# Stepping over neighbouring blocks in the moving operand and the result of the up and down projections

## What is computed

```python
# first block, feed-forward part: D_FF = 2816
h = rms_norm(x, norm_ffn_pre)
u = causal_dwconv(h @ w_up, conv_ffn_w)          # w_up: 1024 x 5632
a, g = jnp.split(u, 2, axis=-1)
f = (jax.nn.gelu(g, approximate=True) * a) @ w_down   # w_down: 2816 x 1024
x = x + rms_norm(f, norm_ffn_post)
...
# second block, feed-forward part: D_FF_2 = 4096
hn = rmsnorm(h, norm_mlp_g)
x = h + jnp.square(jax.nn.relu(hn @ w_up)) @ w_down   # 1024 x 4096 and 4096 x 1024
```

## Time and profile before

| | |
|---|---|
| time, median of 2 runs | 902.34 us (901.83 to 902.85) |
| profiled execution, first to last instruction | 900.7 us |
| PE busy | 888.3 us, 99% |
| PE weight loads busy (beside PE) | 821.5 us, 91% |
| DVE busy | 571.0 us, 63% |
| ACT busy | 496.2 us, 55% |
| POOL busy | 136.0 us, 15% |
| granted TensorE clock, mean | 1.000 |
| DMA | 156.33 MB, mean 174 GB/s |

### The profile page before, as it was taken

The page is one execution under the profiler, slowest core; times in us unless marked ns, Lnnn a source line. Parts: engine busy times, 40 slices in busy tenths (PEclk is TensorE's granted clock), DMA queues, the critical chain, the costliest instruction groups (busy, mean ns, idle before and its releaser), DMA issues.

```text
span 900.7 us, 15634 instructions
## 1 busy us (share of the span) xinstructions
PE 888.3 (99%) x6451; PEld 821.5 (91%) x6451; DVE 571.0 (63%) x824; ACT 496.2 (55%) x771; POOL 136.0 (15%) x151
## 2 busy tenths in 40 slices
PE   8999999999999999999999999999999999999998
PEld 8999999889999988788899988999999899998886
DVE  4556554878888746666767797765467655554542
ACT  5576864556656634566776764423454565554330
POOL 6011101611111100133443110000100011110000
PEclk9999999999999999999999999999999999999999
DMA  7843364665665566346544546542345656656560
GB/s 279 275 155 118 95 227 150 232 207 181 199 199 179 188 210 214 131 169 242 182 141 144 160 133 177 155 135 77 115 140 191 187 168 202 193 187 204 181 200 23
DMA packets 132594, 156.33 MB, mean 174 GB/s; under 512 B 9353, under 2 KB 106028, under 8 KB 132268
## 3 DMA queue, kind: packets, MB, share of 16 engines
q1 hardware_dynamic: 125844, 151.78, 51.9%
q10 hardware_dynamic: 6680, 3.56, 1.3%
HBM read 153.08 MB, written 2.24 MB: 172 GB/s over the span
## 4 chain that ended last, share of the span: by engine, by line
PE 83%; DVE 8%; DMA 3%; ACT 3%; issue 1%; POOL 1%; SPq 0%; ACTq 0%; POOLq 0%
PE ps L1979 72%; PE ps L1934 4%; PE ps L2010 3%; DVE wl L828 2%; PE ps L1931 2%; PE ps L2235 2%; DVE gv L862 1%; DVE gkq L862 1%; DMA U<-blocks 1%; DMA raw<-in_w_in 1%; DMA blocks<-last 1%; DVE mt L1267 1%; DMA Yc<-inverses 1%; ACT wh L1426 1%; DMA inverses<-Y 0%
## 5 line engine op out<-in xcount | busy, mean ns | idle before, releaser
L828 DVE TENSOR_TENSOR wl<-raw,wh 128x1024 fp32r<-128x1024 f32 (+1 forms) x275 | 326.4, 1205 | 190.0 <-ACT wh L1426 189.9
L1979 PE MATMUL ps<-xh,wh 128*128 128x256 f32 x1280 | 357.3, 282 | 0.7 <-ACT xh L1474 0.7
L1979 PE MATMUL ps<-xh,wl 128*128 128x256 f32 x1280 | 350.6, 277 | 0.0
L1426 ACT ACTIVATE wh<-raw 128x1024 fp32r<-128x1024 f32 (+1 forms) x292 | 286.6, 1024 | 115.4 <-PE ps L1979 93.0
L1979 PE MATMUL ps<-xl,wh 128*128 128x256 f32 x1280 | 348.3, 277 | 0.0
L1979 PEld LDWEIGHTS ps<-xh,wh 128*128 128x128 f32 x1280 | 238.9, 188 | 4.5 <-issue 1.4
L1979 PEld LDWEIGHTS ps<-xh,wl 128*128 128x128 f32 x1280 | 238.8, 188 | 0.0
L1979 PEld LDWEIGHTS ps<-xl,wh 128*128 128x128 f32 x1280 | 238.0, 188 | 0.3
L669 POOL TENSOR_TENSOR wl<-raw,wh 128x1024 fp32r<-128x1024 f32 (+1 forms) x17 | 44.2, 2600 | 81.6 <-ACT wh L1426 81.3
L1979 PE MATMUL ps<-wh,f2L 128*128 128x512 f32 x128 | 49.8, 389 | 0.0
L1979 PE MATMUL ps<-wl,f2H 128*128 128x512 f32 x128 | 49.8, 389 | 0.0
(11 more groups left out here) (334 smaller groups left out, 1363.8 us busy)
## 6 DMA issues: line engine op xcount, KB each, us to landing
raw<-in_w_in SPq DMA_DIRECT2D x55, 1024.0 KB, 5.1
raw<-in_w_up SPq DMA_DIRECT2D x38, 1024.0 KB, 5.2
raw<-in_w_down SPq DMA_DIRECT2D x26, 1024.0 KB, 5.0
raw<-in_w_out SPq DMA_DIRECT2D x8, 1024.0 KB, 5.1
raw<-in_w_proj_fox SPq DMA_DIRECT2D x4, 1024.0 KB, 5.1
raw<-in_w_proj_gdn SPq DMA_DIRECT2D x4, 1024.0 KB, 5.1
raw<-in_w_conv_branch SPq DMA_DIRECT2D x4, 512.0 KB, 3.4
raw<-in_w_att_branch SPq DMA_DIRECT2D x4, 512.0 KB, 3.3
```

Of the source, the lines that this page charges most:

```text
L828: e.tensor_tensor(L, R, H.bitcast(F32), ALU.subtract).then_inc(lo.sem)
L1426: e.activation(tile_of(WH, u)[:, k:kc, :], tile_of(RAW, u)[:, k:kc, :], ACT.Copy).then_inc(hi.sem)
L1979: k = e.matmul(o, l, r, start=opens, stop=done and n == ends[c], skip_group_check=True)
```

## The change

In the units of the four feed-forward stages the access patterns of the moving operand `r` and of the result `o` are rearranged, both in the same way: `(b h e)` becomes `h b e`. With h = 2 and e = 16, all even runs of 16 elements (64 bytes) are taken first, then all odd ones. Each column still goes to its own place.

| units | stage | h, e | runs | shape of `r` and `o` |
|---|---|---|---|---|
| 32 to 53 | first up | 2, 16 | 64 bytes | 128 x 2 x 8 x 16 |
| 54 to 62 | first down, without the last three units | 4, 16 | 64 bytes | 128 x 4 x 8 x 16 |
| 114 to 129 | second up | 2, 32 | 128 bytes | 128 x 2 x 4 x 32 |
| 130 to 145 | second down | 2, 8 | 32 bytes | 128 x 2 x 32 x 8 |

The stationary operand, the number and order of instructions on every engine, the waits and the transfers are the same as before.

```diff
@@ in tensor(e), beside unit
+            def strided(ap, h, e):
+
+                return ap.rearrange("p (b h e) -> p h b e", h=h, e=e)
+
+            def order_of(u):
+                if U_UP <= u < U_DN:
+                    return 2, 16
+                if U_DN <= u < AHEAD2[0]:
+                    return 4, 16
+                if U_UP2 <= u < U_DN2:
+                    return 2, 32
+                return (2, 8) if u >= U_DN2 else None
+
@@ in unit
                     W = (H, H, L)[j][:, q, :]
                     cs = slice(c * P, (c + 1) * P)
                     l, r = (W[:, cs], X) if mode == "B" else (X[:, cs], W)
+                    if order_of(u):
+                        o, r = strided(o, *order_of(u)), strided(r, *order_of(u))
                     k = e.matmul(o, l, r, start=opens, stop=done and n == ends[c], skip_group_check=True)
```

## The result

The changed kernel takes 920.57 us (median of 2 runs, 920.25 to 920.88) against 902.34, a ratio of 1.0202 with a 95% interval of 1.0173 to 1.0232. It is 18.2 us slower. That it is slower is clear; whether by more than two per cent is not, since 2% lies inside the interval. The time lies in the stated range, but the forecast was no change.

A forecast was written before the change was run, and what follows sets the result against it. TensorE's matmul pace was taken to bound the kernel. The 900.7 us span plus 337.3 us of touched matmuls times a pace change of zero, with 1.6 us around the span, gave 902.3 us; range 892 to 925 us.

The forecast's parts named there:

- What bounds the kernel: Whole kernel: TensorE busy 888.3 of 900.7 us, never kept waiting in the touched stretches, so matmul pace sets the end.
- The counts of matmuls: Four touched stages: 1056, 192, 768 and 384 matmuls, together 337.3 us, 37% of the span, times any pace change.
- I take zero for all four orders: Four touched stages: a jump in the address costs nothing, giving 902.3 us; no effect had chance 0.50.
- Slower outright: Four touched stages: each jump stops the stream one cycle, 22.4 us more, 924.7 us; chance 0.12.
- Rung (a): Touched matmuls lose a favourable position, 4.5 or 2.3 ns each, up to 9.5 us; within the small loss, chance 0.15.
- The block fetched anew: Second down alone pays for re-entering a fetched 64-byte block, 5.1 us; within the small loss, chance 0.15.
- untouched matmuls keep their pace: Outside the four touched stages: matmuls must run at their old pace in every case.
- The 17th cycle goes: Four touched stages: the extra cycle per 16 columns vanishes, 19.8 us less, 882.5 us; chance 0.07, partial gain 0.10.
- rung (c): Four touched stages: a jump halves the rate, some 330 us more, near 1230 us; chance 0.06.
- The 17th cycle belongs to the element rate: Four touched stages: the extra cycle per 16 columns is float32's element rate, address order free, 902.3 us; chance 0.50.
- Where it is paid: Touched matmuls: a jump's stop could come at the moving operand or at PSUM; no size given to either.

The follow-up runs named there:

- read_only: Against the unchanged kernel, only the moving operand's read is stepped, with the change's four orders; result written in one run: 920.21 us against 902.63, ratio 1.0193.
- small_steps: Against the unchanged kernel, read and result stepped by (4,4) in both up stages and (2,64) in both down stages: 904.75 us against 902.64, ratio 1.0025.
- write_only: Against the unchanged kernel, only the result's write is stepped, with the change's four orders; moving operand read in one run: 902.57 us, ratio 0.9998.

## Why the prediction was wrong, point by point

**What bounds the kernel** was right, and it is why the pace alone decides: the two stretches carry the growth and no wait does. The counts of matmuls and the way of adding them up held to 0.1 us once the measured surpluses are put in: 1056, 192, 768 and 384 times the new surpluses make 18.1 of 18.2 us.

**The step that failed** is "I take zero for all four orders". It rested on matmuls in plain float32 that read in two runs of 512 bytes, and on their durations, whose modelled ends say little about the pace, as the prediction itself notes. The price was not zero but 8.0, 12.7, 6.7 and 5.7 ns a matmul, and read_only showed that the read of the moving operand pays all of it (ratio 1.0193), the write nothing (0.9998). Runs of 512 bytes were later measured in float32r: (2,128), four of them in 512 columns, costs nothing either (226.7 ns), while (2,16) costs 13.3. The row was read rightly and carried too far: from runs of 512 bytes to runs of 32 to 128.

**The rivals.** "Slower outright", one cycle a jump, came nearest in the total, 22.4 us, by accident; it alone put the upper end of the range above the measured time, so that the range held is luck. Its own test refutes it: it asked for 6.7, 13.3, 3.3 and 26.7 ns, the trace has 8.0, 12.7, 6.7 and 5.7, and for small_steps it gives some 50 us more, where 2.1 were measured. Rung (a), 4.5 and 2.3 ns for a lost position, named a thing that exists: a contiguous read moved by 64 bytes pays 6.6 ns. But the rung was priced too low, at 9.5 us in all, and its own sign, the same 2 to 5 ns whatever the length of the run, did not come. For the orders of first up and second up most of the price survives with the stationary read stilled, so a lost position is not shown to be the cause. The block fetched anew would have shown in second down alone, and all four stages paid. The prediction also asked that untouched matmuls keep their pace; a few did not, by chance and not through the change (last section). "The 17th cycle goes" was wrong for every order tried; most of it went only for 512 columns that read at most 32 bytes again and again, 3.4 ns left of 13.3, and for 256 columns 4.9 of 6.7 were left even then. The halved rate, rung (c), happens at 8-byte runs, four times shorter than any of the change. "The 17th cycle belongs to the element rate" was wrong as well: 216.7 ns is possible.

**Where it is paid** I had left open between the moving read and the PSUM write. It is the read, all of it.

**Left open.** Why (2,16) costs 8.0 ns and (4,4) 1.1, why (16,4) costs 24 and (32,4) 13, and why the relative position of two contiguous reads matters with a period of 256 bytes. Why (8,8) has two paces is open as well, and so is how much of second down's 5.7 ns belongs to the step alone. No rule that I tried gives the table. That the read pays is shown; the mechanism in the read is not.

## What to carry to other kernels

Read a moving operand in one contiguous run where TensorE is the bound; for an order that must be stepped, price it by a few units on the chip, since neither the number of jumps nor their length gave the cost. Steps on the PSUM side, in runs of 32 bytes and more, were free here. The price of an order in one unit can be off by 4 ns of 113 and by more for some orders, so the choice is settled by running the whole stage. If single matmuls are to be compared, put the candidates side by side into one kernel, read starts and not durations, and keep controls between them.

## What the runs showed of the hardware that I had not expected

- The pace of one and the same contiguous matmul has two values, 113.3 and 117.8 ns, that hold for dozens of matmuls and change at small plain float32 work between them. Before, 42 from 55.10 took 4.95 us, and the kernel after has an untouched stretch of this kind, 132 from 561.83 in 15.74 us, 119.2 ns each with what surrounds them. It is not an effect of the change: inside that row the kernel before and read_only run at 113.3 ns, the kernel after, write_only and small_steps at 117.8. A matmul of 64 rows ahead of a unit often, not always, brings back 113.3.
- The pace of contiguous reads depends on where the moving and the stationary operand start relative to each other: 113.4 when both are moved by 16, 32 or 48 elements, 117.9 to 120.0 when one is.
- Reading at most 32 bytes again and again streams 512 columns in 216.7 ns; reading one block of 64 bytes again and again is slower, 242.8 ns, than reading 2048 bytes once, 226.7.
